# Interleaving two stationary weight tiles in memory, in every pass whose weights stay in the array

## The chip, the cores and the metric

One core of one Trainium2 chip runs the whole program. Five engines work side by side: TensorE (PE; its loads of the stationary operand are listed apart, as PEld), VectorE (DVE), ScalarE (ACT), GpSimd (POOL) and SyncE (SP). The metric is the time of one execution on the device, in microseconds, and lower is better. The median of three runs stands for a kernel.

## The reference

Two blocks of two layers each work on one sequence of 256 tokens and 1024 features, in float32:

```python
def first_block(...):      # layer 0: gMLP mixer, layer 1: differential attention
    h = h + rmsnorm(mixer(rmsnorm(h, g0)), g1)
    h = h + rmsnorm(conv_ffn(rmsnorm(h, g2)), g3)

def conv_ffn(x, w_up, conv_w, conv_b, w_down):     # D_FF = 2816
    h = causal_dwconv(x @ w_up, conv_w, conv_b)
    g, u = h[..., :D_FF], h[..., D_FF:]
    return (jax.nn.gelu(g) * u) @ w_down

def second_block(...):     # layer 0: pooling mixer, layer 1: stick-breaking attention
    ...
    x = x + rms_norm(sq_relu_mlp(h, w_up, w_down), g)

def sq_relu_mlp(h, w_up, w_down):                  # hidden width 4096
    u = jnp.matmul(h, w_up)
    return jnp.matmul(jnp.square(jax.nn.relu(u)), w_down)
```

Almost all of the arithmetic is in matrix products of the 256 tokens with weights that are read once from memory.

## The kernel before

**Units of weights.** All weights come in 1 MB units of 128 partitions by 2048 float32 numbers (`UNIT`), in the order of their use. SyncE brings them into `raw`. ScalarE rounds a unit to the 32-bit matmul format in `w_hi` (line 316), and VectorE stores the rest that the rounding left in `w_lo` (line 337). The activations are split in the same way, into the halves of `a_hl` and `b_hl`. A product is then three matmuls in one pass each: high with high, high with low, low with high. Where the moving operand can hold both halves of the activations side by side, the first two become one matmul of 512 columns.

**Two kinds of passes.** In the passes that go up in width (the first products of the gated unit, of both feed-forward networks, of both MLPs, the queries and keys of both attentions) the weights are the stationary operand and the activations move. One unit holds 8 blocks `k` of the contraction, and for each of them two tiles `m` of 128 output features. Each matmul is a load of a 128 by 128 stationary tile and then the streaming of 256 or 512 moving columns:

- `unit_pair` (line 685: 512 columns) and the `low_pair` behind it (line 717: 256 columns) are the passes of the networks. `half_pair` (line 708) does the same as line 685 for one half of the tokens, in 256 columns, behind a junction between layers.
- `pair_part` (lines 786 and 788) is the same product in the differential attention, and `unit_feat` and `feat_part` do it by `three` (lines 661 to 663) in 256 columns.

In the other passes (down in width, the values of the attentions, the gating half of the first mixer) the activations are the stationary operand and the weights move. Their units are read in runs of 256 or 512 neighbouring columns.

**Order.** The sequence of instructions of every engine is written out by hand. Semaphores `hi_ready` and `lo_ready` tell TensorE that a unit is split, and `unit_done` gives its buffers back. `up_units`, on the host, lays out the units of the passes that go up.

Of the kernel before, what the change touches and what calls it, by code (L numbers as in the profile page):

```python
# [24 lines left out]
P = 128  # L25
T = 256
D = 1024
DT = D // P
# [7 lines left out]
UNIT = 16 * P  # L36
RAW = 3
CUT = 3
HIGH, LOW = 4, 3
# [43 lines left out]
for _name, _n in (("first_g", DT), ("sub_g", 1), ("conv_b", 2 * 2 * FT), ("conv_w", 2 * 3 * 2 * FT),  # L83
# [5 lines left out]
STICK_UNITS = (("q", 0), ("q", 1), ("k", 0), ("v", 0), ("k", 1), ("v", 1), ("q", 2), ("k", 2), ("v", 2), ("q", 3),  # L89
               ("k", 3), ("v", 3))  # L90
# [28 lines left out]
def build(nc, xT, x_rows, gains, cols, rows, ws, wsT, rel_bias, onehot, line_dram, lines_dram, out):  # L119
    ctx = ExitStack()  # L120
    with ctx:
        def sb(name, shape, dt=F32):
            return ctx.enter_context(nc.sbuf_tensor(name, shape, dt))
# [6 lines left out]
        w_hi = sb("w_hi", [P, HIGH, UNIT], F32R)  # L130
        w_lo = sb("w_lo", [P, LOW, UNIT], F32R)
        x = sb("x", [P, 2, D])
        a_hl = sb("a_hl", [P, DT, 2, T], F32R)
        a_hi, a_lo = a_hl[:, :, 0, :], a_hl[:, :, 1, :]
# [99 lines left out]
        wk = ctx.enter_context(nc.psum_tensor("wk", [P, NB, 2 * T], F32))  # L234
# [167 lines left out]
        def hi_halves(n):  # L402


            return (J_GMLP, J_FFN0, J_DIFF, J_POOL, J_STICK).index(n) + 1 + (n in (J_POOL, J_STICK))
# [252 lines left out]
        def _(pe):  # L658
            def three(o, still, still_lo, moving, moving_lo, first, last):

                pe.matmul(o, still, moving, start=first, stop=False, skip_group_check=True)  # L661
                pe.matmul(o, still, moving_lo, start=False, stop=False, skip_group_check=True)  # L662
                return pe.matmul(o, still_lo, moving, start=False, stop=last, skip_group_check=True)  # L663

            def unit_feat(u, bank, hi=a_hi, lo=a_lo):


                pe.wait_ge(lo_ready, u + 1)
                wh = w_hi[:, u % HIGH, :].rearrange("p (k m) -> p k m", k=DT)
                wl = w_lo[:, u % LOW, :].rearrange("p (k m) -> p k m", k=DT)  # L670
                for k in range(DT):
                    for m in range(2):
                        c = slice(m * P, (m + 1) * P)
                        mm = three(wk[:, bank, m * T:(m + 1) * T], wh[:, k, c], wl[:, k, c],
                                   hi[:, k, :], lo[:, k, :], k == 0 and m == 0, k == DT - 1)
                mm.then_inc(unit_done, 1)

            def unit_pair(u, banks):


                pe.wait_ge(hi_ready, u + 1)
                wh = w_hi[:, u % HIGH, :].rearrange("p (k m) -> p k m", k=DT)
                for k in range(DT):
                    for m in range(2):
                        pe.matmul(banks[:, m, :], wh[:, k, m * P:(m + 1) * P], a_hl[:, k, :, :].rearrange("p e t -> p (e t)"),  # L685
                                  start=k == 0, stop=False, skip_group_check=True)
                low_pair(u, banks)

            def half_there(n, h, k, kv):

                if k % 4 == 0:
                    if kv:
                        pe.wait_ge(blo_ready, 2 * h + k // 4 + 1)
                    else:
                        pe.wait_ge(alo_ready, DT + turn(n, h, k // 4))

            def half_pair(u, banks, n, h, x=a_hl, kv=False, ks=range(DT)):

                if h == 0 and ks == FORE and n != J_MLP0:
                    pe.wait_ge(hi_half_ready, hi_halves(n))  # L700
                elif h == 0:
                    pe.wait_ge(hi_ready, u + 1)
                c = slice(h * P, (h + 1) * P)
                wh = w_hi[:, u % HIGH, :].rearrange("p (k m) -> p k m", k=DT)
                for k in ks:
                    half_there(n, h, k, kv)
                    for m in range(2):
                        pe.matmul(banks[:, m, :].rearrange("p (e t) -> p e t", e=2)[:, :, c], wh[:, k, m * P:(m + 1) * P],  # L708
                                  x[:, k, :, c], start=h == 0 and k == 0, stop=False, skip_group_check=True)

            def low_pair(u, banks, hi=a_hi):

                pe.wait_ge(lo_ready, u + 1)
                wl = w_lo[:, u % LOW, :].rearrange("p (k m) -> p k m", k=DT)
                for k in range(DT):
                    for m in range(2):
                        mm = pe.matmul(banks[:, m, T:2 * T], wl[:, k, m * P:(m + 1) * P], hi[:, k, :],  # L717
                                       start=False, stop=k == DT - 1, skip_group_check=True)
                mm.then_inc(unit_done, 1)

# [42 lines left out]
            def feat_part(u, bank, ks, hi=a_hi, lo=a_lo):  # L763

                if ks[0] == 0:
                    pe.wait_ge(lo_ready, u + 1)
                wh = w_hi[:, u % HIGH, :].rearrange("p (k m) -> p k m", k=DT)
                wl = w_lo[:, u % LOW, :].rearrange("p (k m) -> p k m", k=DT)
                for k in ks:
                    for m in range(2):  # L770
                        c = slice(m * P, (m + 1) * P)
                        mm = three(wk[:, bank, m * T:(m + 1) * T], wh[:, k, c], wl[:, k, c],
                                   hi[:, k, :], lo[:, k, :], k == 0 and m == 0, k == DT - 1)
                if ks[-1] == DT - 1:
                    mm.then_inc(unit_done, 1)

            def pair_part(u, banks, ks):

                if ks[0] == 0:
                    pe.wait_ge(lo_ready, u + 1)  # L780
                wh = w_hi[:, u % HIGH, :].rearrange("p (k m) -> p k m", k=DT)
                wl = w_lo[:, u % LOW, :].rearrange("p (k m) -> p k m", k=DT)
                for k in ks:
                    for m in range(2):
                        c = slice(m * P, (m + 1) * P)
                        pe.matmul(banks[:, m, :], wh[:, k, c], a_hl[:, k, :, :].rearrange("p e t -> p (e t)"),  # L786
                                  start=k == 0, stop=False, skip_group_check=True)
                        mm = pe.matmul(banks[:, m, T:2 * T], wl[:, k, c], a_hi[:, k, :],
                                       start=False, stop=k == DT - 1, skip_group_check=True)
                if ks[-1] == DT - 1:  # L790
                    mm.then_inc(unit_done, 1)
# [162 lines left out]
            for q in range(4):  # L954
                if q == 2:
                    pe.wait_ge(line_copied, 1)
                if q == 3:
                    pe.wait_ge(sd2_ready, 1)
                unit_feat(U_GMLP + 4 + q, q)
                if q == 2:  # L960
                    spatial()
# [9 lines left out]
            def ffn_up(l, base, n, i, a):  # L971
                s = ffn[l]
                if i:
                    pe.wait_ge(s["padded"], 2 * (i - 1) + a + 1)
                unit_pair(ffn_units(base, i)[a], ffn_banks(n, i, a))
# [93 lines left out]
            for j in range(1, 4):  # L1069
                u = U_DIFF + 3 * j  # L1070
# [29 lines left out]
            u = U_DIFF + 12  # L1100
# [15 lines left out]
            wh = w_hi[:, U_POOL % HIGH, :].rearrange("p (g k m) -> p g k m", g=4, k=2)  # L1116
            wl = w_lo[:, U_POOL % LOW, :].rearrange("p (g k m) -> p g k m", g=4, k=2)
# [23 lines left out]
            def mlp_up(l, base, n, i):  # L1141
                pe.wait_ge(mlp[l]["summed"], i - 1)
                unit_pair(mlp_units(base, i)[0], mlp_banks(n, i))
# [135 lines left out]
            u = U_STICK + 12  # L1279
# [951 lines left out]
    return np.where(rel > 0, half, 0) + np.where(n < exact, n, np.minimum(large, half - 1))  # L2231


def up_units(w, tiles):

    t = w.reshape(DT, P, -1, P)[:, :, np.asarray(tiles).reshape(-1), :]
    t = t.reshape(DT, P, -1, 2 * P)
    return np.ascontiguousarray(t.transpose(2, 1, 0, 3)).reshape(-1, P, UNIT)


def down_units(w):

    t = w.reshape(-1, 2, P, D)
    return np.ascontiguousarray(t.transpose(0, 2, 1, 3)).reshape(-1, P, UNIT)
# [74 lines left out]
```

## Time and profile before

| | |
|---|---|
| median of three runs | 1062.55 us (1062.2 to 1063.03) |
| span of the profiled execution, first to last instruction | 1060.2 us |
| TensorE, matmuls | busy 1049.2 us, 99% |
| TensorE, loads of the stationary operand | busy 920.8 us, 87% |
| VectorE | busy 777.2 us, 73% |
| ScalarE | busy 613.8 us, 58% |
| GpSimd | busy 120.7 us, 11% |
| memory traffic | 202.20 MB, mean 191 GB/s |

The profiled execution has no time of its own beside its span. The span is 2.35 us below the median, for what lies ahead of the first instruction and behind the last. A busy share of matmuls near 99% says that TensorE hardly waits, but not that it streams at its peak: matmuls overlap in the records, and their ends are modelled. The distance between the starts of neighbouring matmuls tells more.

### The profile page before, as it was taken

Reading aid. Unit: us, or ns where it says so; the run is one execution under the profiler, and the core shown is the slowest. Engines: PE = TensorE matmul, PEld = TensorE weight load, DVE = VectorE, ACT = ScalarE, POOL = GpSimd, SP = SyncE. Lnnn points to the kernel's source line nnn. Section 1 sums busy time; section 2 is a strip of 40 time slices with the busy share of each in tenths; the row PEclk is TensorE's granted clock in tenths of the full one; section 3 lists DMA queues with packets and bytes.
Section 4 is the critical chain, followed back from the end, with each engine's and each line's share of the span. In section 5 each row is a group of like instructions: output and inputs, shape, how many; then the busy total and the mean of one; then the engine's idle time right before and its main releaser. Section 6 shows DMA issues by size and latency. Waiting matters only on the chain.

```text
span 1060.2 us, 15281 instructions
## 1 busy us (share of the span) xinstructions
PE 1049.2 (99%) x6158; PEld 920.8 (87%) x6158; DVE 777.2 (73%) x928; ACT 613.8 (58%) x840; POOL 120.7 (11%) x115
## 2 busy tenths in 40 slices
PE   9999999999999999999999999999999999999997
PEld 7989888888989898888888988888899979888886
DVE  6878877667887789766778956556687869655654
ACT  7757665557566676665657534344575656534432
POOL 0000432220000004662110000000000000000000
PEclk9999999999999999999999999999999999999999
DMA  8934885563544446576551674555264425665541
GB/s 315 350 143 165 289 301 194 174 213 134 191 170 157 159 158 234 190 253 216 164 195 40 241 294 160 206 191 186 92 254 144 139 101 199 218 204 193 178 179 40
DMA packets 31574, 202.20 MB, mean 191 GB/s; under 512 B 3688, under 2 KB 3856, under 8 KB 9104
## 3 DMA queue, kind: packets, MB, share of 16 engines
q1 hardware_dynamic: 28464, 189.16, 50.4%
q0 software_dynamic: 3040, 12.07, 3.5%
q8 instruction: 49, 0.80, 0.3%
q14 instruction: 21, 0.17, 0.0%
HBM read 200.15 MB, written 2.63 MB: 191 GB/s over the span
## 4 chain that ended last, share of the span: by engine, by line
PE 91%; DVE 7%; ACT 1%; issue 1%; POOL 0%; DVEq 0%; ACTq 0%; POOLq 0%
PE wk L685 22%; PE wk L717 14%; PE acc L661 10%; PE acc L662 10%; PE acc L663 10%; PE wk L661 5%; PE wk L662 4%; PE wk L663 4%; PE wk L708 2%; PE acc L708 1%; PE wk L786 1%; DVE x L1733 1%; DVE w_lo L337 1%; PE acc L717 1%; PE acc L882 1%
## 5 line engine op out<-in xcount | busy, mean ns | idle before, releaser
L337 DVE TENSOR_TENSOR w_lo<-raw,w_hi 128x2048 fp32r<-128x2048 f32 x161 | 369.0, 2297 | 49.5 <-ACT w_hi L316 44.3
L316 ACT ACTIVATE w_hi<-raw 128x2048 fp32r<-128x2048 f32 x166 | 316.4, 1909 | 14.9 <-DMA raw<-ws 10.4
L685 PE MATMUL wk<-a_hl,w_hi 128*128 128x512 f32 x1024 | 243.4, 390 | 0.0
L685 PEld LDWEIGHTS wk<-a_hl,w_hi 128*128 128x128 f32 x1024 | 190.6, 188 | 38.7 <-DVE region L1958 0.2
L661 PE MATMUL acc<-w_hi,b_hl 128*128 128x512 f32 x432 | 169.0, 391 | 0.0
L662 PE MATMUL acc<-w_lo,b_hl 128*128 128x512 f32 x432 | 168.8, 391 | 0.0
L663 PE MATMUL acc<-w_hi,b_hl 128*128 128x512 f32 x432 | 168.2, 389 | 0.0
L717 PEld LDWEIGHTS wk<-a_hl,w_lo 128*128 128x128 f32 x1216 | 155.2, 191 | 5.1
L717 PE MATMUL wk<-a_hl,w_lo 128*128 128x256 f32 x1216 | 158.0, 283 | 0.0
L1617 ACT ACTIVATE region<-wk 128x512 f32<-128x512 f32 x30 | 17.9, 596 | 156.5 <-PE wk L717 156.5
L663 PEld LDWEIGHTS acc<-w_hi,b_hl 128*128 128x128 f32 x432 | 81.2, 188 | 17.2
L661 PEld LDWEIGHTS acc<-w_hi,b_hl 128*128 128x128 f32 x432 | 81.3, 188 | 15.6
L662 PEld LDWEIGHTS acc<-w_lo,b_hl 128*128 128x128 f32 x432 | 81.3, 188 | 15.1
L1968 DVE SCALAR_TENSOR_TENSOR region<-region,prm 128x256 f32<-128x256 f32 x176 | 82.9, 512 | 11.9 <-ACT region L1498 10.3
L2127 DVE TENSOR_TENSOR region<-wk,region 128x512 f32<-128x512 f32 x30 | 20.7, 690 | 90.0 <-ACT region L1617 90.0
L376 POOL TENSOR_TENSOR region<-region 128x512 f32<-128x512 f32 x20 | 53.2, 2659 | 235.8 <-ACT region L1522 235.8
L1486 ACT ACTIVATE region<-wk 128x512 f32<-128x512 f32 x42 | 24.9, 593 | 68.8 <-PE wk L717 68.8
L1498 ACT ACTIVATE region<-region,prm 128x256 f32<-128x256 f32 x88 | 47.7, 590 | 14.1 <-DVE region L1958 14.1
L1958 DVE TENSOR_TENSOR region<-wk,region 128x512 f32<-128x512 f32 x42 | 28.8, 686 | 33.3 <-ACT region L1486 33.1
L708 PE MATMUL wk<-a_hl,w_hi 128*128 128x256 f32 x384 | 49.8, 285 | 0.5 <-DVE a_hl L1783 0.4
L556 POOL DMA_DIRECT2D gain<-gains x13 | 7.4, 575 | 373.4 <-DVE b_hl L2138 189.2
L708 PEld LDWEIGHTS wk<-a_hl,w_hi 128*128 128x128 f32 x384 | 47.5, 191 | 2.1 <-DVE a_hl L1783 1.1
(271 smaller groups left out, 1560.4 us busy)
## 6 DMA issues: line engine op xcount, KB each, us to landing
raw<-ws SPq DMA_DIRECT2D x172, 1024.0 KB, 4.9
gain<-gains POOLq DMA_DIRECT2D x13, 512.0 KB, 5.2
raw<-ws SPq DMA_DIRECT2D x12, 256.0 KB, 6.5
region<-rows SPq DMA_DIRECT2D x1, 1664.0 KB, 11.2
lines_dram<-line_dram POOLq DMA_DIRECT2D x1, 1536.0 KB, 8.1
bias<-gains POOLq DMA_DIRECT2D x3, 512.0 KB, 4.8
region<-xT SPq DMA_DIRECT2D x4, 256.0 KB, 6.1
x<-x_rows SPq DMA_DIRECT2D x1, 1024.0 KB, 8.9
```

The source lines that it names most:

```text
L316: act.activation(w_hi[:, u % HIGH, :], raw[:, u % RAW, :], ACT.Copy).then_inc(hi_ready, 1)
L337: dve.tensor_tensor(low_of(u), raw[:, u % RAW, :], w_hi[:, u % HIGH, :].bitcast(F32), ALU.subtract).then_inc(lo_ready, 1)
L376: eng.tensor_tensor(hf[:, p:p + 2, :], gl[:, p:p + 2, :], cv[:, p:p + 2, 1, :], ALU.mult)\
L661: pe.matmul(o, still, moving, start=first, stop=False, skip_group_check=True)
L662: pe.matmul(o, still, moving_lo, start=False, stop=False, skip_group_check=True)
L663: return pe.matmul(o, still_lo, moving, start=False, stop=last, skip_group_check=True)
L685: pe.matmul(banks[:, m, :], wh[:, k, m * P:(m + 1) * P], a_hl[:, k, :, :].rearrange("p e t -> p (e t)"), start=k == 0, stop=False, skip_gr ...
L708: pe.matmul(banks[:, m, :].rearrange("p (e t) -> p e t", e=2)[:, :, c], wh[:, k, m * P:(m + 1) * P], x[:, k, :, c], start=h == 0 and k == ...
L717: mm = pe.matmul(banks[:, m, T:2 * T], wl[:, k, m * P:(m + 1) * P], hi[:, k, :], start=False, stop=k == DT - 1, skip_group_check=True)
L1498: act.activation(cv[:, p + a, q, :], hb[:, p + a, q, 2:HW], ACT.Identity, scale=w, bias=bb)\
L1958: dve.tensor_tensor(hb[:, p + a, :, 2:HW], ffn_banks(n, i, a)[:, :, 0:T], ffn_low[:, a, :, :], ALU.add)\
L1968: dve.scalar_tensor_tensor(out=cv[:, p + a, q, :], in0=hb[:, p + a, q, tap:tap + T], scalar=prm[:, bass.ds(col, 1)], in1=cv[:, p + a, q, : ...
```

## The change

The stationary tiles of the passes that go up are read with a step of two. Before, a row of a unit held, for each block `k`, first the 128 columns of tile 0 and then the 128 columns of tile 1. Now column 0 of tile 0, column 0 of tile 1, column 1 of tile 0 and so on alternate in memory. The host lays the units out so (`up_units`), except those whose weights move: the values of both attentions, which are named in a new argument. A tile `m` of block `k` is now the elements 256 k + m, 256 k + m + 2, and so on. The number and the order of the instructions, their sizes, their outputs and their semaphores stay as they are on every engine. Here is the diff, with places that repeat the same edit left out:

```diff
+            def still_tiles(w):
+
+                return w.rearrange("p (k j m) -> p k m j", k=DT, m=2)
+
             def unit_feat(u, bank, hi=a_hi, lo=a_lo):
                 pe.wait_ge(lo_ready, u + 1)
-                wh = w_hi[:, u % HIGH, :].rearrange("p (k m) -> p k m", k=DT)
-                wl = w_lo[:, u % LOW, :].rearrange("p (k m) -> p k m", k=DT)
+                wh = still_tiles(w_hi[:, u % HIGH, :])
+                wl = still_tiles(w_lo[:, u % LOW, :])
                 for k in range(DT):
                     for m in range(2):
-                        c = slice(m * P, (m + 1) * P)
-                        mm = three(wk[:, bank, m * T:(m + 1) * T], wh[:, k, c], wl[:, k, c],
+                        mm = three(wk[:, bank, m * T:(m + 1) * T], wh[:, k, m, :], wl[:, k, m, :],
                                    hi[:, k, :], lo[:, k, :], k == 0 and m == 0, k == DT - 1)
...
-                wh = w_hi[:, u % HIGH, :].rearrange("p (k m) -> p k m", k=DT)
+                wh = still_tiles(w_hi[:, u % HIGH, :])
                 for k in range(DT):
                     for m in range(2):
-                        pe.matmul(banks[:, m, :], wh[:, k, m * P:(m + 1) * P], a_hl[:, k, :, :].rearrange("p e t -> p (e t)"),
+                        pe.matmul(banks[:, m, :], wh[:, k, m, :], a_hl[:, k, :, :].rearrange("p e t -> p (e t)"),
                                   start=k == 0, stop=False, skip_group_check=True)
                 low_pair(u, banks)
...
-def up_units(w, tiles):
+def up_units(w, tiles, moving=()):
 
     t = w.reshape(DT, P, -1, P)[:, :, np.asarray(tiles).reshape(-1), :]
-    t = t.reshape(DT, P, -1, 2 * P)
-    return np.ascontiguousarray(t.transpose(2, 1, 0, 3)).reshape(-1, P, UNIT)
+    t = t.reshape(DT, P, -1, 2 * P).transpose(2, 1, 0, 3)
+    paired = t.reshape(-1, P, DT, 2, P).swapaxes(3, 4).reshape(t.shape)
+    keep = np.isin(np.arange(len(t)), moving)[:, None, None, None]
+    return np.where(keep, t, paired).reshape(-1, P, UNIT)
...
-    parts += [up_units(a["b_w_in"][0], qkv_tiles), down_units(a["b_w_out"][0])]
+    parts += [up_units(a["b_w_in"][0], qkv_tiles, range(2, 12, 3)), down_units(a["b_w_out"][0])]
...
-    parts += [up_units(qkv, stick_tiles), down_units(a["w_o_2"][0])]
+    parts += [up_units(qkv, stick_tiles, [c for c, at in enumerate(STICK_UNITS) if at[0] == "v"]), down_units(a["w_o_2"][0])]
```

The same edit stands in `half_pair` (line 708), `low_pair` (717), `feat_part` and `pair_part` (786, 788).

## Rows read from the trace of the kernel before

**Rows 1.** The page's busy times: engine, busy us, share of the span, instructions.
```profile
PE 1049.2 (99%) x6158; PEld 920.8 (87%) x6158; DVE 777.2 (73%) x928; ACT 613.8 (58%) x840; POOL 120.7 (11%) x115
```

**Rows 2.** The page's TensorE clock by slices of the span, in tenths of full speed.
```profile
PEclk9999999999999999999999999999999999999999
```

**Rows 3.** The page's chain that ended last: shares of the span by engine.
```profile
PE 91%; DVE 7%; ACT 1%; issue 1%; POOL 0%; DVEq 0%; ACTq 0%; POOLq 0%
```

**Rows 4.** The chain in order of time: start us, length us, what, count.
```profile
48.41 3.57 PE acc L944 x32
...
119.73 1.91 PE wk L717 x16
...
640.55 3.63 PE wk L685 x16
...
887.32 1.92 PE wk L708 x16
```

**Rows 5.** Groups by line and form: matmuls of 512 columns with weights stationary.
```profile
L685 PE MATMUL wk<-a_hl,w_hi 128*128 128x512 f32 x1024 | 243.4, 390 | 0.0
...
L786 PE MATMUL wk<-a_hl,w_hi 128*128 128x512 f32 x96 | 34.9, 404 | 0.0
```

**Rows 6.** The same view: matmuls of 256 columns with weights stationary.
```profile
L717 PE MATMUL wk<-a_hl,w_lo 128*128 128x256 f32 x1216 | 158.0, 283 | 0.0
L708 PE MATMUL wk<-a_hl,w_hi 128*128 128x256 f32 x384 | 49.8, 285 | 0.5 <-DVE a_hl L1783 0.4
...
L661 PE MATMUL wk<-a_hl,w_hi 128*128 128x256 f32 x96 | 27.5, 287 | 0.0
L662 PE MATMUL wk<-a_hl,w_hi 128*128 128x256 f32 x96 | 27.2, 283 | 0.0
L663 PE MATMUL wk<-a_hl,w_lo 128*128 128x256 f32 x96 | 27.2, 283 | 0.0
L788 PE MATMUL wk<-a_hl,w_lo 128*128 128x256 f32 x96 | 26.9, 281 | 0.0
...
L708 PE MATMUL acc<-a_hl,w_hi 128*128 128x256 f32 x128 | 17.6, 285 | 0.0
...
L662 PE MATMUL wk<-b_hl,w_hi 128*128 128x256 f32 x48 | 13.6, 283 | 0.0
L661 PE MATMUL wk<-b_hl,w_hi 128*128 128x256 f32 x48 | 13.6, 283 | 0.0
L663 PE MATMUL wk<-b_hl,w_lo 128*128 128x256 f32 x48 | 13.6, 283 | 0.0
...
L717 PE MATMUL acc<-a_hl,w_lo 128*128 128x256 f32 x64 | 8.3, 284 | 0.0
...
L708 PE MATMUL acc<-b_hl,w_hi 128*128 128x256 f32 x32 | 4.5, 289 | 0.3 <-DVE b_hl L1795 0.3
...
L717 PE MATMUL acc<-b_hl,w_lo 128*128 128x256 f32 x16 | 2.1, 283 | 0.0
```

**Rows 7.** The same view: loads of 128 and of 64 stationary columns.
```profile
L685 PEld LDWEIGHTS wk<-a_hl,w_hi 128*128 128x128 f32 x1024 | 190.6, 188 | 38.7 <-DVE region L1958 0.2
...
L1196 PEld LDWEIGHTS wk<-region 128*64 128x64 f32 x24 | 1.2, 135 | 0.8
```

**Rows 8.** The timeline around 640 us: start us, us, what.
```profile
640.16 0.39 PE L663 MATMUL acc<-w_hi,b_hl 128*128 128x512 f32 x1
640.17 0.41 PEld L685 LDWEIGHTS wk<-a_hl,w_hi 128*128 128x128 f32 x2
640.39 0.39 PE L685 MATMUL wk<-a_hl,w_hi 128*128 128x512 f32 x1
```

**Rows 9.** Busy us by stretch: us, PE, PEld, DVE, ACT, POOL, clock, DMA share, GB/s.
```profile
640.00:750.00 110.00, 110.00 (x554) 93.94 (x553) 64.08 (x52) 46.24 (x43) 0.00 (x0) 1.00 0.55 191
...
883.00:897.00 14.00, 13.97 (x108) 13.42 (x107) 12.96 (x12) 7.61 (x8) 0.00 (x0) 1.00 0.59 226
```

More of the change, by code:

```diff
@@ L703, in half_pair @@
                 c = slice(h * P, (h + 1) * P)
-                wh = w_hi[:, u % HIGH, :].rearrange("p (k m) -> p k m", k=DT)
+                wh = still_tiles(w_hi[:, u % HIGH, :])
                 for k in ks:
@@ L707, in half_pair @@
                     for m in range(2):
-                        pe.matmul(banks[:, m, :].rearrange("p (e t) -> p e t", e=2)[:, :, c], wh[:, k, m * P:(m + 1) * P],
+                        pe.matmul(banks[:, m, :].rearrange("p (e t) -> p e t", e=2)[:, :, c], wh[:, k, m, :],
                                   x[:, k, :, c], start=h == 0 and k == 0, stop=False, skip_group_check=True)
@@ L713, in low_pair @@
                 pe.wait_ge(lo_ready, u + 1)
-                wl = w_lo[:, u % LOW, :].rearrange("p (k m) -> p k m", k=DT)
+                wl = still_tiles(w_lo[:, u % LOW, :])
                 for k in range(DT):
                     for m in range(2):
-                        mm = pe.matmul(banks[:, m, T:2 * T], wl[:, k, m * P:(m + 1) * P], hi[:, k, :],
+                        mm = pe.matmul(banks[:, m, T:2 * T], wl[:, k, m, :], hi[:, k, :],
                                        start=False, stop=k == DT - 1, skip_group_check=True)
@@ L766, in feat_part @@
                     pe.wait_ge(lo_ready, u + 1)
-                wh = w_hi[:, u % HIGH, :].rearrange("p (k m) -> p k m", k=DT)
-                wl = w_lo[:, u % LOW, :].rearrange("p (k m) -> p k m", k=DT)
+                wh = still_tiles(w_hi[:, u % HIGH, :])
+                wl = still_tiles(w_lo[:, u % LOW, :])
                 for k in ks:
                     for m in range(2):
-                        c = slice(m * P, (m + 1) * P)
-                        mm = three(wk[:, bank, m * T:(m + 1) * T], wh[:, k, c], wl[:, k, c],
+                        mm = three(wk[:, bank, m * T:(m + 1) * T], wh[:, k, m, :], wl[:, k, m, :],
                                    hi[:, k, :], lo[:, k, :], k == 0 and m == 0, k == DT - 1)
@@ L780, in pair_part @@
                     pe.wait_ge(lo_ready, u + 1)
-                wh = w_hi[:, u % HIGH, :].rearrange("p (k m) -> p k m", k=DT)
-                wl = w_lo[:, u % LOW, :].rearrange("p (k m) -> p k m", k=DT)
+                wh = still_tiles(w_hi[:, u % HIGH, :])
+                wl = still_tiles(w_lo[:, u % LOW, :])
                 for k in ks:
                     for m in range(2):
-                        c = slice(m * P, (m + 1) * P)
-                        pe.matmul(banks[:, m, :], wh[:, k, c], a_hl[:, k, :, :].rearrange("p e t -> p (e t)"),
+                        pe.matmul(banks[:, m, :], wh[:, k, m, :], a_hl[:, k, :, :].rearrange("p e t -> p (e t)"),
                                   start=k == 0, stop=False, skip_group_check=True)
-                        mm = pe.matmul(banks[:, m, T:2 * T], wl[:, k, c], a_hi[:, k, :],
+                        mm = pe.matmul(banks[:, m, T:2 * T], wl[:, k, m, :], a_hi[:, k, :],
                                        start=False, stop=k == DT - 1, skip_group_check=True)
```

## The prediction

> **What bounds the kernel now.** I read the busy times first. TensorE's matmuls are busy for 99% of the span and VectorE for 73% [rows 1], so the question is what a matmul costs. The chain that ended last says the same: 91% of it lies on TensorE and 7% on VectorE [rows 3]. The clock is at its top tenth in every slice, and 1.00 in the stretches that I looked at [rows 2, 9], so the engine is at its 2.4 GHz level, and no matmul is slow for want of clock.
>
> The average durations of matmuls (390 ns, 283 ns) overlap and are of no use. The chain in order of time gives the spacing from start to start. Sixteen matmuls of 512 columns take 3.63 us, or 226.9 ns each. Sixteen of 256 columns take 1.91 to 1.92 us, or 119.4 to 120.0 ns each [rows 4]. At 2.4 GHz the streaming alone takes 512 / 2.4 = 213.3 ns and 256 / 2.4 = 106.7 ns. So each matmul has a surplus of 13.6 ns or 12.7 to 13.3 ns, and it is the same for both widths. It therefore belongs to the matmul or to its load, not to the columns that stream.
>
> The loads come next. A load starts just as the matmul ahead of it starts: at 640.17 us the load, at 640.16 us the matmul of the tile before, and at 640.39 us the matmul that uses the load [rows 8]. It is thus hidden behind one matmul. How fast loads can follow each other is seen where matmuls are too narrow to hide them: 32 matmuls of 128 columns take 3.57 us, or 111.6 ns each, though streaming takes 53.3 ns [rows 4]. That is the floor that loads set. The duration of a load agrees: 188 ns for 128 columns and 135 ns for 64 [rows 7], so 53 ns for 64 columns, 106 ns for 128, and the rest is latency. Against this floor a 512-column matmul leaves 226.9 - 111.6 = 115 ns of slack for its load, and a 256-column matmul only 119.7 - 111.6 = 8 ns (119.7 is the middle of the two rows).
>
> **What the change touches.** No instruction is added, removed or moved, on any engine: the sequences with their waits are identical but for line numbers. Transfers have the same size, and ScalarE and VectorE split a unit as one run of 2048 elements as before, so the order of the columns is nothing to them. Outputs go to the same places in the same form. The units whose weights move keep their layout. All that differs is the step of the stationary read, in these loads:
>
> - behind 512 columns: 1024 + 96 = 1,120 [rows 5]
> - behind 256 columns: line 717 has 1216 + 64 + 16 = 1,296, line 708 has 384 + 128 + 32 = 544, lines 661 to 663 have 3 x 96 + 3 x 48 = 432, line 788 has 96, together 2,368 [rows 6]
>
> That is 3,488 of 6,158 loads [rows 1].
>
> **What a load with a step of two costs.** No row of before has one, so I bound it. The lower bound of a cost is nothing: 128 elements are fetched at the rate of before. The upper bound is that memory is fetched in pieces of two neighbours or more and half of each piece is now wasted, at a rate that was just enough before: the floor doubles to 2 x 111.6 = 223.2 ns. Behind 512 columns this still costs nothing, since 223.2 is under 226.9. Behind 256 columns each matmul would then take 223.2 instead of 119.7 ns, 103.5 ns more.
>
> I take the lower bound, and choose by the moving read, the nearest row. It passes over 512 elements of 4 bytes in 226.9 ns: 9.0 bytes per ns in each partition. The load passes over 128 elements in 111.6 ns: 4.6 bytes per ns. With a step of two it passes over 9.2 bytes of memory per ns, of which it uses half. TensorE's other read already does that pace all the time, with matmul upon matmul. If both reads fetch pieces of one size, the load has the room. That they are built alike is my assumption.
>
> The Trainium skill has a rule for this, in "Advanced Engine Details and Errata", section "SBUF Cachelines": memory is accessed in lines of 16 bytes, full speed needs accesses that stay in a line, and at least two hits on each line to absorb the latency. With 4-byte elements a step of two makes exactly two hits, so by the page the load costs what it did, and the sum is zero; a step of four would not be free by it. No row here shows a stepped load, so the trace neither bears the rule out nor speaks against it.
>
> The sum: 1,120 x 0 + 2,368 x 0 = 0 us. The span stays at 1060.2 us, and with the 2.35 us that lie between it and the median, the time stays at **1062.5 us**. Up to 8 ns more per load would be hidden entirely. Where TensorE has waited, at the start of some of the 3,488 / 16 = 218 passes, nothing hides the load; there it would have to be slower by 10 ns in every one of them to make 2.1 us, 0.2% of the time, which is about the least that a measurement of this kernel tells from no change.
>
> **Rival 1: the load takes its fetches from the moving read (slower).** The surplus of 13.6 ns is the same at both widths. It may be the time for which a load's fetches hold up the streaming matmul beside it. If this goes by the stretch of memory that the load passes over, it doubles: 13.6 ns more for each of 3,488 matmuls, 47.4 us, and the time is 1,110 us. For it speaks that the surplus doesn't grow with the columns. Against it speaks that a fixed cost of passing from one matmul to the next would look the same. It decides as soon as the load costs the neighbour more than 2.1 us / 3,488 = 0.6 ns.
>
> **Rival 2: the load's own fetch slows down (much slower).** The floor doubles as bounded above: 2,368 x 103.5 = 245.1 us, and the time is 1,308 us. It would show only behind 256 columns. The point from which it decides is a floor above 119.7 ns; a load that slows by half (167 ns) costs 2,368 x 47.7 = 113 us. For it speaks that the load streams at only half the pace of the moving read (4.6 against 9.0 bytes per ns), so its path may be narrower, in which case it has no room. Against it speaks that this pace can as well be a limit of the array's side, which a step does not touch.
>
> **Rival 3: the surplus goes (faster).** If neighbouring elements fetched by the load one after the other from the same piece of memory are what collides with the moving read, spreading them over twice the stretch could relieve it. At most the whole surplus goes behind 512 columns, 1,120 x 13.6 = 15.2 us, and behind 256 columns the 8.1 ns down to the load's floor, 2,368 x 8.1 = 19.2 us. Together 34.4 us, and the time is 1,028 us. Half of that effect gives 1,045 us. For it speaks only that the surplus exists, at both widths alike, and has no other explanation in the trace. Nothing shows that it depends on addresses. VectorE would soon limit such a gain in the stretches behind junctions, where it is busy 12.96 of 14 us, though not in the long ones, at 64.08 of 110 us [rows 9].
>
> **How the numbers follow.** No change: 0.53. Rival 1 or a smaller form of it: 0.14. Rival 2 in whole or in part: 0.13. Rival 3 in whole or in part: 0.20, a good deal for a case with so little behind it, because the surplus is unexplained and every matmul carries it. Faster by over 0.2% is rival 3, slower rivals 1 and 2, 0.27 together. The range must hold 8 in 10: it takes in no change, rival 3 to its end at 1,028 us and rival 1 to its end at 1,110 us, 0.87 in all, and leaves out rival 2, which begins to matter in steps of tens of microseconds.
>
> **What the profile of the changed kernel would show.** Right: in the chain, sixteen matmuls of line 685 again in 3.63 us and sixteen of 717 in 1.91 to 1.92 us, and loads of 188 ns. Rival 1: sixteen in some 3.85 us and 2.13 us, so both widths longer by the same amount, while the down passes (lines 661 to 663 in 512 columns) stay. Rival 2: line 685 unchanged, 717 and 708 at 3.57 us for sixteen, and loads near 295 ns. Rival 3: both shorter, 3.41 and 1.79 us. The prediction is wrong if the stepped loads cost or give back anything that the next matmul has to wait for, by more than 8 ns behind 256 columns, or if they change the surplus at all.

## The result, and the profile after

The changed kernel takes 1069.49 us (1069.2 to 1070.39, four runs) against 1062.58 us of the kernel before in the same session. The ratio is 1.0066 with an interval of 1.0054 to 1.0078: slower by 7 us. The forecast was no change. The time lies in the range of 1028 to 1110 us, but the interval of the ratio leaves out no change, which was held to be the likeliest case.

The page's busy times after answer to [rows 1]. TensorE moved by 6.2 us of matmuls and 6.7 us of loads, the other engines by 1.2 us or less:

```profile
PE 1055.4 (99%) x6158; PEld 927.5 (87%) x6158; DVE 777.0 (73%) x928; ACT 615.0 (58%) x840; POOL 120.9 (11%) x115
```

The chain in order of time of the changed kernel (start us, length us, what, count) answers to [rows 4]. Line 685 is now line 688, and 717 is 720:

```profile
645.45 3.73 PE wk L688 x16
649.18 1.91 PE wk L720 x16
```

Sixteen matmuls of 512 columns take 3.73 us where they took 3.63 us, so 233.3 ns each in place of 226.7. Sixteen of 256 columns still take 1.91 us. The groups by line and form say the same for the whole program (columns as in [rows 5] and [rows 6]; the number ahead of the comma is busy us):

```profile
L688 PE MATMUL wk<-a_hl,w_hi 128*128 128x512 f32 x1024 | 250.2, 395 | 0.0
...
L720 PE MATMUL wk<-a_hl,w_lo 128*128 128x256 f32 x1216 | 158.1, 282 | 0.0
L711 PE MATMUL wk<-a_hl,w_hi 128*128 128x256 f32 x384 | 49.9, 285 | 0.4 <-DVE a_hl L1784 0.4
L787 PE MATMUL wk<-a_hl,w_hi 128*128 128x512 f32 x96 | 34.8, 402 | 0.0
```

One line moved: the 1,024 matmuls of `unit_pair` are busy 250.2 us in place of 243.4, which is 6.8 us and so all of the loss. (The page's sum rises by 6.2 us only, since the 30 matmuls that warm the array up at the start were busy 4.8 us in this execution and 6.3 us in the one of before.) The 256-column matmuls have what they had (158.1 for 158.0, 49.9 for 49.8). So have the 96 matmuls of 512 columns of `pair_part`, which alternate with matmuls of 256 (34.8 for 34.9). The stepped loads last a little longer: 194 ns in place of 188 behind 512 columns, 195 in place of 191 behind 256 (line 720).

```profile
L688 PEld LDWEIGHTS wk<-a_hl,w_hi 128*128 128x128 f32 x1024 | 196.9, 194 | 38.7
L720 PEld LDWEIGHTS wk<-a_hl,w_lo 128*128 128x128 f32 x1216 | 156.0, 195 | 5.3
```

### The profile page after: what moved, and what is told of

It is laid out like the page before. It is cut to its first block, busy times and chain, and to the rows that moved or that the text cites. A ratio compares the mean times of both kernels' runs of the same rounds, so it can differ in the third digit from the quotient of the medians.

```text
span 1067.5 us, 15281 instructions
## 1 busy us (share of the span) xinstructions
PE 1055.4 (99%) x6158; PEld 927.5 (87%) x6158; DVE 777.0 (73%) x928; ACT 615.0 (58%) x840; POOL 120.9 (11%) x115
## 4 chain that ended last, share of the span: by engine, by line
PE 90%; DVE 7%; ACT 1%; issue 1%; DMA 0%; POOL 0%; SPq 0%; DVEq 0%; ACTq 0%; POOLq 0%
PE wk L688 22%; PE wk L720 14%; PE acc L661 10%; PE acc L662 10%; PE acc L663 10%; PE wk L661 5%; PE wk L662 4%; PE wk L663 4%; PE wk L711 2%; PE acc L711 1%; PE wk L787 1%; DVE x L1734 1%; DVE w_lo L337 1%; PE acc L720 1%; PE acc L883 1%
## 5 line engine op out<-in xcount | busy, mean ns | idle before, releaser
L688 PE MATMUL wk<-a_hl,w_hi 128*128 128x512 f32 x1024 | 250.2, 395 | 0.0
L688 PEld LDWEIGHTS wk<-a_hl,w_hi 128*128 128x128 f32 x1024 | 196.9, 194 | 38.7
L720 PE MATMUL wk<-a_hl,w_lo 128*128 128x256 f32 x1216 | 158.1, 282 | 0.0
L711 PE MATMUL wk<-a_hl,w_hi 128*128 128x256 f32 x384 | 49.9, 285 | 0.4 <-DVE a_hl L1784 0.4
L711 PEld LDWEIGHTS wk<-a_hl,w_hi 128*128 128x128 f32 x384 | 47.7, 195 | 1.9 <-DVE a_hl L1784 0.9
```

Source lines behind the costliest of these rows:

```text
L688: pe.matmul(banks[:, m, :], wh[:, k, m, :], a_hl[:, k, :, :].rearrange("p e t -> p (e t)"), start=k == 0, stop=False, skip_group_check=True)
L720: mm = pe.matmul(banks[:, m, T:2 * T], wl[:, k, m, :], hi[:, k, :], start=False, stop=k == DT - 1, skip_group_check=True)
```

## The experiments

Two theories stood at first. In one, a stepped load holds up the stream beside it. In the other, the load itself takes longer. Both left open why only the 512-column matmuls pay. Of the twelve kernels below eight are variants of the whole program. Four are probes, which leave the whole computation out: runs of 16 to 64 of the same matmuls follow each other with nothing beside them.

```
for i in range(48):      # one source line for each width and step
    pe.matmul(acc[:, i % 2, 0:512], at(step, i % 16), mv[:, 0:512], ...)
# at(step, i): tile i of 128 stationary columns with that step; mv: the moving operand
```

### 1. Where in the kernel does the cost lie?

Both variants are the changed kernel, with the step of two only in a part of the units:

```diff
+def stepped(u):
+    return (u in WIDE_UPS) == True      # the second variant: == False
...
+                if stepped(u):
+                    return w.rearrange("p (k j m) -> p k m j", k=DT, m=2)
+                return w.rearrange("p (k m j) -> p k m j", k=DT, m=2)
```

`WIDE_UPS` are the units that `unit_pair` reads, and the host lays out the others contiguously. For the first variant was expected:

> Step of two only in the units that unit_pair reads (the networks' first products behind the first three units of each phase); all others contiguous as before. If the cost lies behind the 512-column matmuls alone, this run has the whole of it: 1024 x 6.7 ns = 6.9 us, 1069.4 us, ratio 1.0065. Rival (the cost is spread over all loads, about 2 ns each): these units hold 2,048 of 3,488 loads, so 4.1 us, 1066.6 us.

It took 1069.2 us against 1062.27 us, ratio 1.0063 (1.005 to 1.0075). For the second:

> The complement: step of two in all weight-stationary units but those of unit_pair. If the cost lies behind the 512-column matmuls of unit_pair alone: 1062.6 us, no change. If it is spread over all loads: 1,440 x 2 ns = 2.8 us, 1065.4 us.

It took 1062.58 us against 1062.27 us, ratio 1.0 (0.9991 to 1.0009). Here is the group of `unit_pair` in the first and in the second variant:

```profile
L710 PE MATMUL wk<-a_hl,w_hi 128*128 128x512 f32 x1024 | 250.1, 395 | 0.0
```

```profile
L710 PE MATMUL wk<-a_hl,w_hi 128*128 128x512 f32 x1024 | 243.4, 390 | 0.0
```

So the units of `unit_pair` carry the whole loss, and 1,440 stepped loads elsewhere cost nothing that can be measured. A cost spread over all loads is refuted.

### 2. A step of four

```diff
-                return w.rearrange("p (k j m) -> p k m j", k=DT, m=2)
+                return [w.rearrange("p (a j b m) -> p a b m j", a=DT // 2, b=2, m=2)[:, k // 2, k % 2] for k in range(DT)]
```

> The change with a step of four (two blocks k and their two tiles m interleaved), in the same passes. By the page's rule each access now meets another 16-byte line, so the load slows by more than a few ns: if the load's time doubled (223 ns) behind 256 columns, 2,368 x 103 ns = 245 us, 1308 us. If the cost goes by the number of lines that the load touches (32, 64, 128 at steps 1, 2, 4) and is 6.7 ns for 32 more lines, it is 20 ns behind 512 columns: 1024 x 20 = 20 us, 1083 us. If only an odd or even step matters: 1069.5 us as with two.

It took 1330.49 us, ratio 1.2524 (1.2507 to 1.2541), 268 us more. Its loads (the number ahead of the second bar is the mean in ns) took 327 ns in place of 191 behind 256 columns, and 310 in place of 188 behind 512:

```profile
L720 PEld LDWEIGHTS wk<-a_hl,w_lo 128*128 128x128 f32 x1216 | 289.8, 327 | 0.0
L688 PEld LDWEIGHTS wk<-a_hl,w_hi 128*128 128x128 f32 x1024 | 245.7, 310 | 1.5
```

Behind 256 columns the spacing went from 120.0 to 233.3 ns, behind 512 to about 238 ns. Neither of the cheaper theories, 1083 and 1069.5 us, holds. This is the upper bound of the prediction, at one step further: the load's own floor doubled (section 3) and passed the stream. For the load it agrees with the rule of "Advanced Engine Details and Errata", section "SBUF Cachelines", of the Trainium skill: at two hits on a 16-byte line little is lost, at one hit much more. The moving operand does not follow the rule of the lines: at a step of two, still two hits on a line, a matmul already takes twice as long (section 4).

### 3. The floor of a load, and the widths

> A probe that leaves the whole computation out (its output is a copy of a slice of the weights): runs of 64 matmuls, each with its own load, for moving widths 64, 128, 192, 256, 320, 384, 448 and 512 and a stationary read with a step of 1, 2, 4, 8 and 16 elements. Nothing else reads or writes memory beside them. It reads the spacing of matmuls at each width and step. What the changed kernel has shown: 226.7 ns became 233.3 ns behind 512 columns, 120 ns stayed 120 ns behind 256. Theory A (the stepped load holds up the stream beside it by a fixed time, and behind 256 columns this was hidden since there the load and not the stream sets the spacing): step 2 adds about 6.7 ns at 320, 384, 448 and 512 columns alike, and the spacing at 64 and 128 columns stays at 112 ns. Theory B (the stepped load takes longer by itself): 64 and 128 columns go from 112 to 118 ns, and the wide ones gain the same 6.7 ns. Theory C (the cost comes from the other engines' traffic in the kernel): this probe shows 227 ns at 512 columns for step 1 and 2 alike. By the page's rule of 16-byte lines a step of 4 should cost much more than a step of 2, and 8 and 16 no more than 4.

Read from the starts of the records, the spacing at steps 1 and 2 was 120 and 120 ns behind 256 columns, 146.7 and 146.7 behind 320, 173.3 and 173.3 behind 384, 226.7 and 233.3 behind 512. At step 4 it was 233.3 ns from 64 to 384 columns. So the cost of step 2 is there without any traffic of other engines (theory C falls), and it is neither the same at all wide widths (A) nor there at 384 (B). The narrow widths could not be read at full clock, since the granted clock fell. This row of its busy times by stretch (us, PE, PEld, ACT, POOL, clock, DMA share, GB/s) shows it in the runs of 64 and 128 columns:

```profile
60.00:120.00 60.00, 60.00 (x269) 60.00 (x270) 0.00 (x0) 0.00 (x0) 0.50 0.00 1
```

The narrow widths tell something else. At the clock of 0.50 (the 1.2 GHz level) a contiguous load and one with a step of two both leave 213.3 ns, about twice the 111.7 ns of full clock, but a step of four leaves 233.3 ns, the same as at full clock. So the floor of a contiguous load goes with TensorE's clock, and the floor at a step of four does not.

The second probe kept wide matmuls between the narrow ones.

> A second probe without the computation, at full clock throughout (narrow matmuls stand between runs of wide ones). The first probe left open why a step of two costs 6.7 ns behind 512 columns and nothing behind 256, 320 and 384. Theory A (the two reads meet at addresses: with a step of two the load passes over memory at the pace of the stream, so the cost hangs on where both start): with the moving operand's start shifted by 8 bytes to 1 KB, or with a load that repeats one tile, the spacing at 512 columns changes between 227 and 233 ns or more, and differs between tile 0 and tile 1. Theory B (the load itself takes 6.7 ns longer, whatever the addresses): the load's floor, read at 64 and 128 columns at full clock, is 112 ns at step 1 and about 118 ns at step 2, and all starts and tiles at 512 columns give 233 ns. Theory C (the cost belongs to a full 512-column matmul, the limit of a bank): 510, 508 and 504 columns show none of it, at 226 ns and below, step 1 and 2 alike. A step of three touches up to 96 lines with 1.33 elements each: by the page's rule (two hits on a line) it costs as much as four at the floor, by the number of lines three quarters of it.

Its chain in order of time. L158, L162, L166 and L170 are 64 columns with steps 1, 2, 3 and 4 of the stationary read. L66 and L68 are 384 columns with steps 1 and 2, L90 and L92 are 504, L102 and L104 are 512. L106, L118 and L130 are 512 columns at step 1 with the moving operand's start 8, 64 and 512 bytes later, and L120 is L118 at step 2:

```profile
26.87 8.35 PE acc L66 x48
35.22 8.32 PE acc L68 x48
...
143.47 10.90 PE acc L90 x48
154.37 10.88 PE acc L92 x48
...
209.16 10.90 PE acc L102 x48
220.06 11.20 PE acc L104 x48
231.26 7.46 PE acc L106 x32
...
276.00 7.33 PE acc L118 x32
283.33 7.47 PE acc L120 x32
...
320.40 7.26 PE acc L130 x32
...
418.35 1.71 PE acc L158 x16
...
425.60 1.80 PE acc L162 x16
...
432.93 2.66 PE acc L166 x16
...
441.12 3.55 PE acc L170 x16
```

The floor of a load is in the last four. A piece of sixteen holds 15 full distances, since a wide matmul follows the last one almost at once. From the starts they are 111.7, 117.8, 175.6 and 233.6 ns at steps 1 to 4. From two on this is 58.4 to 58.9 ns for each unit of step. At a step of one the floor is set elsewhere, since by that measure 58.4 ns would do for the fetches. At a step of two the fetches have just become the slower part, by 6.1 ns. A step of three costs three quarters of a step of four, as by the number of lines touched; that it would be as dear as four is refuted.

The wide ones: 11.20 / 48 = 233.3 ns at 512 columns and step 2, 10.90 / 48 = 227.1 at step 1, and no difference at 384 and 504. So theory B explains the floor but not the cost. L106 is new: with a contiguous load, 512 columns also take 7.46 / 32 = 233.1 ns once the moving operand starts 8 bytes later. A start of 512 bytes later restores 226.9 (L130). At step 2 no start gave less than 231.6 ns. So addresses count, as theory A had it. Where it failed is that repeating tile 0 or tile 1 made no difference at a given step. Theory C, that the cost belongs to a full 512 columns, fails too: 510 columns went from 226.7 to 233.3 ns. Nor is it the alternation of two banks of the output: in the fourth probe all matmuls of 512 columns into one bank took 226.6 ns at step 1 and 233.3 at step 2 again.

### 4. What the surplus is not

> A third probe without the computation. The second probe gave a load floor of 111.5, 117.9, 175.6 and 233.5 ns at steps 1 to 4, which is 58.4 ns for each unit of step from two on, and a surplus over the stream of 13.3 ns (step 1) and 20 ns (step 2) behind 512 columns. Open is whether the surplus is what the load's fetches take from the stream. Theory A (it is: surplus by the stretch of memory that a load passes over, in shares of 32 lines of 16 bytes): a load of 66 columns at step 1 leaves 213.3 + 7 = 220 ns behind 512 columns, 66 columns at step 2 leave 227 ns as 128 columns at step 1 do, and a load that reads one element for all 128 columns leaves 214 to 216 ns. Theory B (the surplus is the passing from one matmul to the next and has nothing to do with fetches): 227 ns in all of these, with 233 ns only where the step is two. For the moving operand: if both reads fetch alike, 58.4 ns per 128 elements and unit of step, a stream with a step of two keeps its pace of 213 ns + surplus or slows to 2 x 4 x 58.4 = 467 ns for 512 columns; if it is served twice as fast as the load, it keeps it.

In the third probe L66 and L68 are 512 columns with steps 1 and 2, L70 has a load of 66 columns, L82 a load that reads one element 128 times. L120 and L122 are 512 moving columns with a step of 2 and 4 in the moving operand. L132 and L134 alternate 512 and 256 columns at steps 1 and 2:

```profile
26.24 7.26 PE acc L66 x32
33.50 7.47 PE acc L68 x32
40.97 7.38 PE acc L70 x32
...
85.53 7.40 PE acc L82 x32
...
179.22 10.88 PE acc L120 x24
190.09 11.07 PE acc L122 x24
...
217.90 5.55 PE acc L132 x32
223.46 5.55 PE acc L134 x32
```

At 512 columns a load with next to nothing to fetch gives 7.40 / 32 = 231 ns, more than a full contiguous one with 227, and one of 66 columns 230.6. That is neither theory A (214 to 220) nor theory B (227). So there the surplus of 13.4 ns is not the fetches of the load added up, and rival 1's price by the stretch of memory fails. Behind 256 columns the same light loads, of 66 columns or of one element, gave 116.7 ns in place of 120.0, so there less to fetch did help. The alternating pair is as long at step 2 as at step 1, 5.55 us, as it was in `pair_part`. A step in the moving operand is dear at once: 453 and 461 ns for 512 columns, about 113 and 115 ns for 128 elements. At a step of two the load needs 117.8 ns for 128 elements, nearly the same. Only at a step of four are the two reads far apart, 115 against 233.6 ns.

### 5. Which address counts

> A fourth probe without the computation. The third probe refuted that the load's fetches make the surplus: a load that reads a single element leaves 231 ns behind 512 columns, and one of 66 columns 231 ns. It showed something else: with the moving operand's start shifted by 16 or 64 bytes, 256 columns with a contiguous load take 113.3 ns in place of 120.0, but 512 columns take 231 and 229 ns in place of 226.7. This probe sweeps the start in steps of 16 bytes. Theory A (only the moving operand's address counts, by its place in a row of 128 or 256 bytes): the pattern repeats with a period of 64, 128 or 256 bytes, and a shift of the stationary tile alone changes nothing. Theory B (the distance between the two operands counts): a shift of the stationary tile by 16 or 64 bytes gives 113 ns as well, and a shift of both by the same amount gives 120 ns. In either case a start that gives 113 ns behind 256 and 227 ns behind 512 columns would make a kernel faster than both: 2,368 x 6.7 ns = 15.8 us.

In the fourth probe L66 and L68 are 512 and 256 columns at the aligned start, L82 and L84 the same with the moving operand 64 bytes later. L194 and L196 have the stationary tile 64 bytes later, L198 both (256 columns):

```profile
26.59 5.44 PE acc L66 x24
32.03 2.87 PE acc L68 x24
...
60.10 5.50 PE acc L82 x24
65.60 2.72 PE acc L84 x24
...
278.69 5.60 PE acc L194 x24
284.28 2.73 PE acc L196 x24
287.01 2.86 PE acc L198 x24
```

At 256 columns, 64 bytes of shift give 113.3 ns in place of 120 whichever operand is shifted (2.72 and 2.73 us), and a shift of both gives 119.7 again (2.86 us). Here the distance between the two operands counts, theory B of this run.

Shifts of 32 and 128 bytes of both gave 120.0 and 119.8 ns and agree. A shift of 16 bytes does not: both together gave 118.4 ns and not 120, and the stationary tile alone left 512 columns at 226.7 ns, while no moving start that lay 16 to 240 bytes off went below 228.9. Nor does the pattern simply repeat every 256 bytes: a moving start 64, 320 or 1,088 bytes later gave 113.3 ns behind 256 columns, one 576 or 832 bytes later 117.8. So the distance is the larger part of the rule and not the whole. It is the steady spacing that changes; that each pair of reads then meets in memory in the same way again and again is an inference.

The best distance for 256 columns is not the best for 512 (5.44 us aligned, 5.50 with the moving operand shifted, 5.60 with the stationary one). The same start could settle at another spacing in another probe (113.3 and 116.7 ns for 16 bytes), so what ran before has a say as well.

### 6. The same in the kernel, without any step

Four variants of the kernel before, all loads contiguous. The control has the padding and the edits that make room for it, and X = 0. The others move one tensor inside its padding by X elements, `a_hl` by 8 or 16, and in the last one `w_lo` by 16, padded in the same way:

```diff
-        a_hl = sb("a_hl", [P, DT, 2, T], F32R)
+        a_hl = sb("a_hl", [P, 64 + DT * 2 * T], F32R)[:, X:X + DT * 2 * T].rearrange("p (k e t) -> p k e t", k=DT, e=2)
...
-        warm = sb("warm", [P, T], mybir.dt.bfloat16)
+        warm = sb("warm", [P, P], mybir.dt.bfloat16)
...
-            keep_warm(wk[:, 0, 0:T], PREWARM)
+            keep_warm(wk[:, 0, 0:P], 2 * PREWARM)
```

> Control for the three runs with it: the kernel before with its contiguous tiles, 256 bytes of padding behind a_hl, and the matmuls that warm the array up at the start in 60 of 128 columns in place of 30 of 256 (this frees the memory). Both theories: 1062.5 us, no change.

The control took 1063.9 us against 1062.4 us, ratio 1.0015 (1.0006 to 1.0025). It should have cost nothing. The steady spacings did not move (line 685 is busy 243.5 us for 243.4, line 717 158.0 for 158.0). In the profiled execution, whose span is 2.9 us longer, 2.4 us of this stand in five places: two early waits for `w_lo`, two gaps around 600 us, and a wait for VectorE near 783 us. At the fourth, near 604 us, TensorE waits for nothing that the profile shows, and it does so in all four kernels with the 30 further matmuls at the start (a row of the control's timeline: start us, length us, what, and idle time ahead of it):

```profile
604.12 0.47 PE L661 MATMUL acc<-w_hi,b_hl 128*128 128x512 f32 x1 [0.55 <-issue]
```

> As the control, but a_hl, the moving operand of the passes in question, starts 32 bytes later. No load has a step. Theory A (the two reads meet at addresses, and a step of two is one way to disturb the favourable meeting): behind 512 columns the spacing goes from 226.7 to about 233.4 ns as in the probe, 1,120 x 6.7 = 7.5 us more; behind 256 columns it is 116.7 to 120 ns, 0 to 7.8 us less. The decisive reading is the spacing of the unit_pair matmuls. Theory B (the slower load of a step of two is needed for the cost): 226.7 ns stay, 1062.5 us.

It took 1066.17 us, ratio 1.0036 (1.0023 to 1.0049). Its chain:

```profile
642.94 3.74 PE wk L685 x16
646.68 1.89 PE wk L717 x16
```

```profile
L685 PE MATMUL wk<-a_hl,w_hi 128*128 128x512 f32 x1024 | 249.8, 396 | 0.6 <-DVE region L2127 0.5
...
L717 PE MATMUL wk<-a_hl,w_lo 128*128 128x256 f32 x1216 | 155.1, 280 | 0.0
```

The first row is the decisive one. Without any step, sixteen 512-column matmuls take 3.74 us, as with the step of two (3.73), only because the moving operand starts 32 bytes later. The matmuls of line 685 lose 6.4 us by it, and those of line 717 win 2.9 us back. Against the control the whole is 2.3 us slower.

> As the control, but a_hl starts 64 bytes later. Theory A, by the probe: behind 512 columns 229 ns, 1,120 x 2.3 = 2.6 us more; behind 256 columns 117.8 ns where the moving row changes with k as it does here, 2,368 x 2.2 = 5.2 us less, at best 113.3 ns and 15.9 us less. So 1060 us, at best 1049 us. Theory B: 1062.5 us.

It took 1060.54 us, ratio 0.9985 (0.9976 to 0.9994). Line 685 lost 2.7 us and line 717 won 5.5 us. Against the control the whole is 3.4 us faster.

> As the control, but w_lo starts 64 bytes later, which shifts the stationary tile of line 717 alone and leaves the distance of w_hi to a_hl. Theory A: the 512-column matmuls of line 685 keep 226.7 ns, the 1,296 of line 717 go to 117.8 ns (2.9 us less) or 113.3 ns (8.7 us less), and the 512-column matmuls of the down passes whose moving operand is w_lo (about 600 of line 662) lose 0 to 6.7 ns each, 0 to 4 us more: 1054 to 1064 us. Theory B: 1062.5 us.

It took 1068.21 us, ratio 1.0057 (1.0044 to 1.0071), outside what was expected. Against the control it is 4.3 us slower:

```profile
L685 PE MATMUL wk<-a_hl,w_hi 128*128 128x512 f32 x1024 | 245.2, 391 | 0.0
...
L717 PE MATMUL wk<-a_hl,w_lo 128*128 128x256 f32 x1216 | 155.8, 281 | 0.0
```

Line 717 won only 2.2 us. Line 685 lost 1.7 us against the control, though its distance was meant to stay. The starts show how. From the ninth matmul of a pass on the spacing is 226.4 to 227.0 ns, as in the control. But the first eight distances take 231.9 ns on average and 228.7 in the control, which is 64 x 8 x 3.2 ns = 1.6 us. So a pass needs some matmuls until its spacing has settled, and here it needs more of them. The padding behind `w_lo` also puts `a_hl` 256 bytes further from `w_hi`, and the down pass ahead of it has another spacing. Which of the two lengthens the settling was not separated. In the kernel with the step of two the pass never settles at 226.7: from its second distance on it stays at 233 to 235 ns.

All three lines of the down passes lost 1.6 to 1.9 us each, not only the one that reads `w_lo`. The other two read `w_hi` and `b_hl`, which lie where they lay in the control, and take turns with it one by one. So a matmul with another distance between its operands also lengthens its neighbours.

### 7. A version that beats both

```diff
+        a_hl = sb("a_hl", [P, 64 + DT * 2 * T], F32R)[:, 16:16 + DT * 2 * T].rearrange("p (k e t) -> p k e t", k=DT, e=2)
...
+        warm = sb("warm", [P, P], mybir.dt.bfloat16)
...
+                    pe.matmul(bank.rearrange("p (e t) -> p e t", e=2), warm[:, :], warm[:, :].unsqueeze(1).broadcast_to([P, 2, P]), start=True, stop=True,
```

> The version that the runs point to: the kernel before with contiguous tiles, a_hl 64 bytes later in memory, and the 30 matmuls that warm the array up in 256 columns as before (their moving operand now reads 128 columns twice, which frees the memory for the shift). Theory A (addresses): the spacings of the run with 64 bytes repeat, 229 to 230 ns behind 512 columns and 114 to 118 ns behind 256. If the control's 1.5 us came from its other way of warming up, this run is faster than the 64-byte run by as much, 1059 us; if not, it repeats its 1060.5 us. Theory B: 1062.4 us.

It took 1058.55 us (1058.01 to 1059.18), ratio 0.9962 (0.9949 to 0.9976): 4.1 us faster than the kernel before and 10.9 us than the changed one. Its chain, and the two groups:

```profile
649.90 3.68 PE wk L685 x16
653.58 1.81 PE wk L717 x16
```

```profile
L685 PE MATMUL wk<-a_hl,w_hi 128*128 128x512 f32 x1024 | 246.0, 393 | 0.4 <-DVE region L1958 0.4
...
L717 PE MATMUL wk<-a_hl,w_lo 128*128 128x256 f32 x1216 | 152.5, 278 | 0.0
```

Line 717 is busy 5.5 us less than before and line 685 2.6 us more. This run is 2.0 us below the one with 64 bytes and the other way of warming up, which is the only difference between them; so the control's 1.5 us most likely lay there too. The idle 0.55 us of the control near 604 us is not in this trace. By what path the 30 further matmuls at the start cost this is not shown.

## Why the prediction was wrong

**What bounds the kernel** was right: the loss came from nothing but the spacing of matmuls, and every other engine kept its busy time to 1.2 us. That the surplus over the stream is the same at all widths holds for 256 and 512 columns (13.3 and 13.4 ns) but not in between: the second probe has 16.0 ns at 448 and 16.7 at 504 columns, with contiguous loads.

**The count of loads** was right, and that instructions, transfers and splits stay too.

**The choice of the lower bound for the load itself** was nearly right. The floor rose from 111.7 to 117.8 ns, by 6.1 ns, within the 8 ns of slack that were read behind 256 columns, and so 2,368 loads cost nothing. The estimate compared 9.2 bytes per ns that a stepped load would need with 9.0 that the moving read has. The load's path turns out to give 128 x 4 bytes in 58.4 ns, or 8.8 bytes per ns, which is just under the need. So the pace that was taken from the moving read was nearly right: at a step of two both reads pass over about 9 bytes per ns (4,096 bytes in 453 ns, 1,024 in 117.8 ns). That they are built alike, as was assumed, does not hold beyond that: at a step of four the moving read takes 115 ns for 128 elements and the load 233.6.

**The step that failed** is "Behind 512 columns this still costs nothing, since 223.2 is under 226.9", and with it the term 1,120 x 0. It treats the load and the stream as two lanes of which the longer one sets the spacing. At 512 columns the floor is 117.8 ns and the slack over 100 ns, and still each matmul of `unit_pair` takes 6.7 ns more: 1,024 x 6.7 = 6.9 us, measured 6.9. The other 96 of the 1,120 cost nothing. What the runs show in its place is that a hidden load can set the spacing of the matmuls beside it by its addresses and by its step. The contiguous load at the aligned start has the shortest spacing of all that were tried at 512 columns, 226.7 ns, and a step of two ends it, as a shift by 32 bytes does. The prediction had named this case in its last words, "or if they change the surplus at all". That the time still fell into the range is no merit of the mechanism: the range had been drawn wide for rivals 1 and 3.

**Rival 1** named the right kind of mechanism, a load that takes something from the stream beside it, and the right sign. Its price was wrong: 13.6 ns for each of 3,488 loads from the stretch of memory passed over, where 6.7 ns for 1,024 was measured, and the third probe refuted the reckoning by the stretch at 512 columns. **Rival 2** was wrong for a step of two and right, to its size, for a step of four: 245 us forecast for a doubled floor, 268 us measured. **Rival 3**, a surplus that can be relieved by other addresses, fell for this change, though its idea made the last version faster.

**What stays open.** That a shift of 32 bytes and a step of two cost the same 6.7 ns suggests one mechanism and does not prove it. Most settled spacings are a whole number of times 6.67 ns, in which 16 columns stream at 2.4 GHz: 113.3, 120.0, 146.7, 173.3, 226.7 and 233.3 ns are 17, 18, 22, 26, 34 and 35 of them. The step of two moved the 512 columns by just one. Not all fit (202.7 ns at 448 columns, 229 with the start 64 bytes later), and no run explains it. Why 512, 510 and 496 columns pay for a step of two (6.7, 6.7 and 5.3 ns in the second probe) and 504, 508 and 384 do not is not explained. Nor is why an alternation of 512 and 256 columns is free of it. That the two reads contend for shared parts of memory is argued from the effect of the distance; no run showed the contention itself.

## What to carry to other kernels

A load that is hidden behind a matmul is not always free: its addresses and its step can still lengthen the distance to the next matmul by several ns, so where thousands of matmuls stand back to back, read the steady spacing of each form and not only whether the longer of the two lanes changes. When a layout changes, look at the spacing at once, and try the start addresses of the two operands: 64 bytes of shift were worth 4 us here, and 32 bytes cost nearly as much (2.3 us against the control). A step of two in float32 stationary tiles is nearly free for the load itself (6 ns), a step of four costs as much again as the load (122 ns).

## What the runs showed that I had not expected

- The start of the moving operand, seen from the stationary one, changes the steady spacing: 113.3 to 120.0 ns at 256 columns, 226.7 to 236.5 ns at 512, for shifts of 0 to 240 bytes. A shift of 256 bytes changed nothing once the spacing had settled (120.0 and 226.7 ns).
- A step in the moving operand doubles the matmul at two (453 ns for 512 columns) and adds little more at four (461 ns), while a step in the load adds 6, 64 and 122 ns at two, three and four.
- Long runs of matmuls of 64 and 128 columns went with a fall of the granted clock from 1.00 to 0.50, the 1.2 GHz level, though TensorE never idled. It fell again in the runs of 192 columns with a step of four, at 234 ns from start to start.
- At the clock of 0.50 a contiguous load takes twice as long, 213.3 ns, and one with a step of four the same 233.3 ns as at full clock.
